# Delta stage: a tile's q, k, v and z in three transfers, three slots for solved blocks, the last substitution spread over the rounds

## What is computed

```
def step(S, inp):
    qc, kc, vc, gc, bc = inp
    decay = jnp.exp(jnp.where(incl, gc[..., :, None] - gc[..., None, :], -jnp.inf))
    kbeta = kc * bc[..., None]
    a = jnp.where(strict, jnp.einsum('bhid,bhjd->bhij', kbeta, kc) * decay, 0.0) + eye
    rhs = jnp.concatenate([vc * bc[..., None], kbeta * jnp.exp(gc)[..., None]], axis=-1)
    sol = lax.linalg.triangular_solve(a, rhs, left_side=True, lower=True, unit_diagonal=True)
    u, w = sol[..., :DV], sol[..., DV:]
    v_new = u - jnp.einsum('bhck,bhkv->bhcv', w, S)
    attn = jnp.einsum('bhid,bhjd->bhij', qc, kc) * decay
    o = (jnp.einsum('bhck,bhkv->bhcv', qc * jnp.exp(gc)[..., None], S)
         + jnp.einsum('bhij,bhjv->bhiv', attn, v_new))
    g_last = gc[..., -1]
    S = (S * jnp.exp(g_last)[..., None, None]
         + jnp.einsum('bhck,bhcv->bhkv', kc * jnp.exp(g_last[..., None] - gc)[..., None], v_new))
    return S, o
```

## Time and profile before

| | |
|---|---|
| time, median of 3 runs | 5176.89 us (5173.43 to 5181.04) |
| profiled execution, its own time | 5176.11 us |
| its span in the trace | 5174.5 us |
| delta stage in the trace | first instruction 854.28, next stage's first transfer 1353.15 us |
| TensorE products, busy share of the whole span | 86% |
| VectorE, ScalarE, POOL | 36%, 31%, 15% |

### The profile page before, as it was taken

How to read it: one execution, slowest core, us unless ns; L and a number is a source line. 1 busy time by engine, 2 the same in 40 slices (tenths; PEclk the granted TensorE clock), 3 DMA queues, 4 the chain that set the end, 5 groups by cost and what they waited for, 6 DMA issues and landing times. The chain is left out here.

```text
span 5174.5 us, 84659 instructions
## 1 busy us (share of the span) xinstructions
PE 4428.8 (86%) x33347; PEld 4164.1 (80%) x33347; DVE 1882.2 (36%) x2633; ACT 1627.9 (31%) x2867; POOL 778.8 (15%) x567
## 2 busy tenths in 40 slices
PE   5799995767696999899778888479999999999994
PEld 4789995666695999898545668369999999999993
DVE  3455664544212000111112222234445454455454
ACT  2574331434322000122102222144334344444441
POOL 0234310211232232133000003100000000000001
PEclk6899997988897999999888558689999999999996
DMA  1223487445431122234010002175556666676675
GB/s 42 59 71 96 132 221 173 116 110 128 117 115 54 62 69 67 67 105 126 31 46 1 0 0 65 70 204 164 155 163 174 172 179 176 176 197 178 178 210 176
DMA packets 1048766, 600.88 MB, mean 116 GB/s; under 512 B 184465, under 2 KB 1006194, under 8 KB 1048578
## 3 DMA queue, kind: packets, MB, share of 16 engines
q1 hardware_dynamic: 984114, 524.46, 36.7%
q10 hardware_dynamic: 55344, 46.60, 3.1%
q0 software_dynamic: 9120, 27.24, 1.7%
HBM read 498.56 MB, written 99.26 MB: 116 GB/s over the span
## 5 line engine op out<-in xcount | busy, mean ns | idle before, releaser
L2247 DVE TENSOR_TENSOR experts_w<-experts_raw,experts_w 128x1024 fp32r<-128x1024 f32 x352 | 415.4, 1221 | 153.6 <-ACT experts_w L2207 153.5
L182 PE MATMUL experts_pa<-experts_hx,experts_w 128*128 128x264 f32 (+6 forms) x1408 | 413.0, 293 | 9.1 <-DVE experts_w L2247 9.1
L183 PE MATMUL experts_pa<-experts_hx,experts_w 128*128 128x264 f32 (+6 forms) x1408 | 411.5, 292 | 0.0
L184 PE MATMUL experts_pa<-experts_hx,experts_w 128*128 128x264 f32 (+6 forms) x1408 | 410.4, 291 | 0.0
L182 PE MATMUL experts_pd<-experts_hid,experts_w 128*128 128x264 f32 (+6 forms) x1408 | 410.2, 291 | 0.0
L183 PE MATMUL experts_pb<-experts_hx,experts_w 128*128 128x264 f32 (+6 forms) x1408 | 409.6, 291 | 0.0
L182 PE MATMUL experts_pb<-experts_hx,experts_w 128*128 128x264 f32 (+6 forms) x1408 | 409.2, 291 | 0.0
L183 PE MATMUL experts_pd<-experts_hid,experts_w 128*128 128x264 f32 (+6 forms) x1408 | 408.9, 290 | 0.0
L184 PE MATMUL experts_pb<-experts_hx,experts_w 128*128 128x264 f32 (+6 forms) x1408 | 408.7, 290 | 0.0
L184 PE MATMUL experts_pd<-experts_hid,experts_w 128*128 128x264 f32 (+6 forms) x1408 | 408.6, 290 | 0.0
L182 PE MATMUL proj_pm<-hT,proj_w_hi 128*128 128x384 f32 (+1 forms) x1152 | 389.6, 338 | 18.4 <-POOL proj_w_lo L622 18.4
(11 more groups left out here) (383 smaller groups left out, 10365.2 us busy)
## 6 DMA issues: line engine op xcount, KB each, us to landing
experts_raw<-in_moe_w SPq DMA_DIRECT2D x352, 512.0 KB, 4.7
experts_raw<-in_moe_w SPq DMA_DIRECT2D x128, 704.0 KB, 6.0
projected<-proj_out SPq DMA_DIRECT2D x48, 544.0 KB, 4.1
proj_w<-in_gdn_w_in ACTq DMA_DIRECT2D x48, 512.0 KB, 4.1
ffnup_w<-in_ffn_w SPq DMA_DIRECT2D x44, 512.0 KB, 4.9
ffndown_w<-in_ffn_w SPq DMA_DIRECT2D x32, 704.0 KB, 4.7
mixout_w<-in_gdn_w_out SPq DMA_DIRECT2D x32, 512.0 KB, 4.1
hidden<-ffnup_hid ACTq DMA_DIRECT2D x22, 544.0 KB, 2.7
```

The costliest lines, as they stand in the source:

```text
L182: pe.matmul(out, as_r(w_hi), as_r(x_hi), start=first, stop=False)
L183: pe.matmul(out, as_r(w_hi), as_r(x_lo), start=False, stop=False)
L184: return pe.matmul(out, as_r(w_lo), as_r(x_hi), start=False, stop=last)
L2247: dve.tensor_tensor(as_r(w[:, u, 1, x, 0:KD, :]), raw[:, x, u, 0:KD, :], w[:, u, 0, x, 0:KD, :], ALU.subtract).then_inc(split[x][u], 1)
```

## The change

- TT, BT and their semaphores get three slots (`AHEAD`), taken by c modulo 3; between and solved blocks of chunk c+3 instead of c+2 are loaded in round c, between ahead of solved. Three clearings stand at the start.
- `load_tile` issues three transfers, v, q with k, and z, each 16 heads of 128 frames, in runs of 512 bytes, into tiles that hold all heads. Tile 0 and the sample's state are issued by ScalarE at its start, the other tiles by SyncE as before.
- POOL's `stage` copies a chunk's v and k (k twice, by a broadcast read) into kst and vst, which now hold two chunks; v and k are turned from there. The products with the state read k and q in the new tile, the gate reads z there.
- The last group's substitution is cut into eight pieces of two rows, one in each of rounds 0 to 7, at VectorE's x0. It is stored in round 11.
- `delta_chunks` is written with a lag between the chains, which is 0.
- The stage has nine more semaphores.

The diff, cut to its core:

```
-def substitute(dve, step, blocks, solved, terms, groups):
+def substitute(dve, step, blocks, solved, terms, groups, first=1, end=SUB):
...
-    for i in range(1, SUB):
+    for i in range(first, end):
...
+LAG = 0
+AHEAD = 3
...
+    n = len(ORDER)
+    for at in range(-n, n * (NCHUNK + 1) + LAG * CHAINS):
+        for ch in range(CHAINS):
+            now, step = divmod(at - LAG * ch, n)
+            run(ch, now, ORDER[step])
...
+        qk, v, z = (st.sb(n, [P, 2, HV, P]) for n in ("qk", "v", "z"))
+        kst, vst = each("kst", [P, 2, PAIRS, 2, CHUNK]), each("vst", [P, 2, HC, CHUNK])
...
-        BT = st.sb("BT", [P, 2, L, HK, CHUNK])
-        TT = st.sb("TT", [P, 2, 2, HK, CHUNK])
+        BT = st.sb("BT", [P, AHEAD, L, HK, CHUNK])
+        TT = st.sb("TT", [P, AHEAD, 2, HK, CHUNK])
...
+            def load_tile(eng, t):
+                par, n = t % 2, TILES[t][1]
+                for to, first, loaded in ((v, 2 * HK, v_loaded), (qk, 0, qk_loaded), (z, 2 * HK + HV, z_loaded)):
+                    eng.dma_start(to[:, par, :, 0:n], proj[first:first + HV, :, t * P:t * P + n].rearrange("h p t -> p h t")).then_inc(loaded[par], 16)
...
+                load_between(0)
                 load_solved(0)
-                load_between(0)
-                load_tile(0)
-                load_solved(1)
-                load_between(1)
                 load_own(0)
-                load_own(1)
                 src = m["block_dram"].rearrange("a k hp i g f -> (a k hp i) g f")
                 sp.dma_start(blocks[:, 0, :, :].rearrange("p j i -> p (j i)"), src[:, NT - 1, :]).then_inc(blocks_loaded, 16)
-                load_tile(1)
...
+                load_between(1)
+                load_solved(1)
+                load_own(1)
+                load_between(2)
+                load_solved(2)
+                load_tile(sp, 1)
                 for c in range(NCHUNK):
                     if c and c % 2 == 0:
                         for ch in C:
                             sp.wait_ge(sems[ch]["o_gated"], PRE + c)
                         store_out(c // 2 - 1)
                         if c // 2 + 1 < NT:
-                            load_tile(c // 2 + 1)
+                            load_tile(sp, c // 2 + 1)
+                    if c == LAST - 2 - AHEAD:
+                        sp.wait_ge(flip_ready, PRE + 1)
...
+                    if c + AHEAD < NCHUNK:
+                        load_between(c + AHEAD)
+                        load_solved(c + AHEAD)
                     if c + 2 < NCHUNK:
-                        load_solved(c + 2)
-                        load_between(c + 2)
                         load_own(c + 2)
...
+                    t = tile(c)
+                    pool.wait_ge(v_loaded[t], landed(c))
+                    if c >= 2:
+                        pool.wait_ge(e["v_turned"], PRE + c - 1)
+                        pool.wait_ge(e["k_turned"], PRE + c - 1)
+                    pool.tensor_copy(vst[ch][:, c % 2, :, :], v[:, t, HC * ch:HC * ch + HC, cols(c)]).then_inc(e["v_staged"], 1)
+                    pool.wait_ge(qk_loaded[t], landed(c))
+                    pool.tensor_copy(kst[ch][:, c % 2, :, :, :], qk[:, t, HK + PAIRS * ch:HK + PAIRS * ch + PAIRS, cols(c)].unsqueeze(2).broadcast_to([P, PAIRS, 2, CHUNK])).then_inc(e["k_staged"], 1)
...
+                load_tile(act, 0)
+                for ch in C:
+                    act.dma_start(S[ch][:, 1, :, :], io["state_delta"][0, 0, HC * ch:HC * ch + HC].rearrange("h k v -> k h v")).then_inc(sems[ch]["state_loaded"], 16)
...
-                substitute(dve, step, blocks, solved, terms, 1)
-                dve.tensor_copy(flipped[:, 0, :, :], solved[:, 0, :, :].rearrange("p r c -> p c r")).then_inc(flip_ready, 1)
+                def last_group(ch, c, l):
+                    if ch or l or not 1 <= c <= SUB // 2:
+                        return
+                    if c == 1:
+                        dve.wait_ge(blocks_loaded, PRE + 16)
+                    substitute(dve, step, blocks, solved, terms, 1, 2 * c - 1, min(2 * c + 1, SUB))
+                    if c == SUB // 2:
+                        dve.tensor_copy(flipped[:, 0, :, :], solved[:, 0, :, :].rearrange("p r c -> p c r")).then_inc(flip_ready, 1)
```

## The result

The changed kernel takes 5030.74 us (median of four runs, 5026.76 to 5039.29) against 5176.15 of the kernel before beside it (5173.43 to 5181.04): a ratio of 0.972, 95% interval 0.9703 to 0.9737. 5034.0 us had been forecast. The profiled execution of after took 5030.56 us with a span of 5028.9, 145.6 less than that of before.

A forecast was written before the change was run, and what follows sets the result against it. Late solved blocks, queued behind tiles on SyncE, stall TensorE, which otherwise bounds the delta rounds. The terms -117.1 - 2.3 - 28 + 4 + 1.3 sum to -142.1, taking 5176.1 to 5034 us, range 5020 to 5075.

The forecast's parts named there:

- What bounds the kernel: Delta stage: TensorE waits for late solved blocks behind tile issue on SyncE; rounds without the stall are bound by TensorE.
- (a): Delta rounds, three slots for solved and between blocks: all 15 waits go, intervals 276.7 instead of 393.8 us, -117.1.
- The seventh cold restart: Last stretch of the delta stage, from 1307.15 us: TensorE's restart at a lower clock goes too, -2.3 us.
- (f): Nine more semaphores, set and cleared: at most 0.16 us each, twice; 0 to 2.9 us, taken as +1.3.
- (b): SyncE's tile in three transfers: issue takes 12 to 14 us, taken as 13, instead of 16.65; none on the path.
- the new runs do nothing, and the sum stands: Rival on SyncE's tile issue: it stays at 16.65 us and the forecast sum holds; no chance of its own given.
- The loads keep the pace: Rival, chance 0.14: queue, landing or contention bring SyncE's pair of rounds above 37 us; 5064 us.
- (c): Regrouping on POOL: four copies a round, 0.62 us each, cost 0 as long as one takes less than about 2 us.
- The rival by which copies set the round: POOL's chain, 9.6 + 4t, passes 18.5 us at 2.2 us a copy; 5202 us at 5 us; chance 0.04.
- (d): Substitution spread over rounds 0 to 7 on VectorE: multiplies blocked by POOL cost 0 to 9 us, taken as +4.
- (e): Stage start: VectorE no longer delays TensorE, while ScalarE issues tile 0 and state; gain 20 to 33 us, taken as -28.
- The signs: Delta-stage trace: x0 of chunk 1 near 885, chunk 16 near 1166, intervals 18.0 to 19.5 us, no wait above 2.

The follow-up runs named there:

- e3: The changed kernel with all 15 steps of the last group's substitution again ahead of VectorE's first step, blocks still loaded early; 5047.84 us.
- e8: The changed kernel with ScalarE issuing only v and qk of tile 0, z and the state following on SyncE; 5030.26 us, ratio to before 0.9719.
- e1: The kernel before with three slots for solved and between blocks, loads three chunks ahead, and nothing else of the change; 5074.91 us.
- e9: The changed kernel with each of a tile's three transfers cut into two half tiles, so runs of 256 bytes; 5045.10 us.
- e6: The changed kernel with each regrouping copy on POOL done five times in a chain; 5067.33 us.
- e5: The changed kernel with each spread piece of the substitution done three times; 5053.56 us.
- e2: The changed kernel with two slots again (AHEAD 2), all the rest of the change kept; 5114.29 us.

## Why the prediction was right, step by step

**What bounds the kernel** held. The 15 waits were those of the second slot: with three slots and nothing else 110.3 us of the stage go, with everything but the slots waits of 6 to 12 us stay.

**(a)** -117.1 forecast, -114.5 measured. The 2.6 us are mostly four rounds that are longer than 18.43 (19.79, 19.42, 19.03 and 18.71). The first three hold a gap in the middle of d0 for which the trace names no engine (1.09, 0.73 and 0.34 us):

```profile
946.47 0.27 PE L1067 MATMUL delta_bank_x<-delta_TT,delta_X 64*64 64x64 f32 x2 [1.09 <-issue]
```

They come ahead of chunks 5, 9 and 13; e3 and e8 have their longer intervals at the same chunks, and one more ahead of chunk 15. No run was made on their cause; it stays open. The seventh cold restart (-2.3 forecast) lies between X(15) and the landing of the last outputs: 38.90 us before, 37.22 after, 1.7 less, and the granted clock over the first 18 us of it is 0.90 before and 1.00 after. The 0.9 by which the last stretch grows behind that landing belong to (f).

The **cover** that (a) rests on was counted too generously. I put SyncE's pair at 18 us plus the tile: 34.6 with the old tile. Three slots alone gave 38.4 to 40.1 with a tile of 16.0 to 17.3, short runs 37.0 to 42.6 with one of 15.0 to 15.9. So what lies beside the tile is 22.3 us on average in e1 and 23.6 in e9, not 18: behind a tile `BT` takes 0.9 to 2.9 us to issue and 16 pieces 7.5 to 10.3 in these two kernels, where I had put 0.5 and 7.44. With this the tile's 16.65 us would not have fitted, and (b) is part of the gain.

**(b)** The issue of a tile takes 8.3 to 9.8 us, less than my 13; of what it saves, `BT` and the pieces behind it take back 2 to 3 (25.3 on average beside the tile in after, 22.3 and 23.6 with the long tiles). The pair takes 34.3 where I had 31. v lands 9.0 and qk 11.3 us behind their issue, as put down. The rival "the new runs do nothing, and the sum stands" fell in its second half: had they done nothing, short runs show what follows, 10.0 us more in the rounds and 7.3 at the start. "The loads keep the pace" was nearer than its 14% said: its mechanism is that of e1 and e9, and after escapes it by the 1.7 to 4.4 us that SyncE stands idle in a pair.

(The text speaks of 18 transfers for a tile's q, k, v, z; there are 16, as the kernel's description says. No number hangs on it.)

**(c)** A copy takes 612 ns, forecast 0.62, and costs nothing:

```profile
L1025 POOL COPY delta_kst<-delta_qk 128x512 f32<-128x512 f32 x34 | 20.8, 612 | 4.2 <-DMA delta_qk<-projected 4.2
L1023 POOL COPY delta_vst<-delta_v 128x512 f32<-128x512 f32 x34 | 20.8, 612 | 2.7 <-DMA delta_v<-projected 2.7
```

The waits of 4.2 and 2.7 us are the start's; no copy waits in the rounds. The rival by which copies set the round was right in its mechanism and too dear by 2.2 us in its constant (e6).

**(d)** +4 forecast, 0 measured. The collision is there, as one piece of after in VectorE's list and POOL's beside it show:

```profile
997.79 4.08 POOL L1033 TENSOR_TENSOR delta_S<-delta_S,glast 128x1024 f32<-128x1024 f32 x2 [9.89 <-PE delta_bank_s L1097]
...
1000.14 0.33 DVE L425 TENSOR_REDUCE delta_solved<-delta_terms 128x13 f32<-128x169 f32 x1
1000.50 1.72 DVE L424 TENSOR_TENSOR delta_terms<-delta_solved,delta_blocks 128x196 f32<-128x196 f32 x1
1002.25 0.36 DVE L425 TENSOR_REDUCE delta_solved<-delta_terms 128x14 f32<-128x196 f32 x1
1002.65 1.41 DVE L1239 SCALAR_TENSOR_TENSOR delta_out<-delta_bank_s,gains,delta_z 128x512 f32<-128x512 f32 x2
1003.97 1.27 DVE L1189 TENSOR_TENSOR delta_TT<-delta_TT,delta_bank_x 128x512 f32<-128x512 f32 x2
```

The second multiply takes 1.72 us where e3, with POOL idle, has 0.49. So it is with the second multiply of each round from 0 to 6, 1.56 us for 4 elements to 1.72 for 196. The first one is not held but holds POOL: in rounds 0 to 7, as it grows from 0.15 to 0.54 us, the two scalings beside it grow from 3.78 to 4.18, and in round 8, without a piece, they take 3.75. Blocked once, for the second scaling, and not for a copy as well, a piece ends 1.2 to 1.4 us later, and the cover just holds that: in round 6 some 0.2 us of it are left (e5). So the term's place was right and its size lay at its lower bound: e3, without the pieces, has rounds of 279.48 against 279.28. (The rule of the Trainium skill, "SBUF — State Buffer", "Who interferes with whom", that such a pair excludes each other for a whole instruction, agrees with the 1.72 us here; the +9 that I derived from it does not, since the exclusion fell on time that nobody was waiting for.)

**(e)** -28 forecast, -29.75 measured, but the reason given was not the one that held. I had x0 at 864.5 and ScalarE busy issuing until 870.5. In after x0 waited for its own block until 874.10, 15.82 us behind the first clearing, while ScalarE was through with issuing at 872.50 and its first copy, at 875.26, waited for nothing but x0. What held x0 was the landing: 16 engines at a share of 1.10 [the third stretch above] with two queues full, and pieces that took 6.5 us to land instead of the 1.8 of the earlier trace rows. Two errors of about 5 us met: x0 later than thought, ScalarE off the path. The first copy, put down for 16.2 us behind the first clearing, came at 17.0, but held by x0 and not by ScalarE's issuing. That the landing is what delays x0 is seen against before and e1, where tile 0 is not on ScalarE's queue: there the 16 pieces had landed 9.7 us behind the first clearing, in after only at 15.6. e8, with 2 MB less, moves x0 by only 1.75 us, and by 1.2 to 1.4 against e2, e3, e5 and e6, which have after's queue (15.2 to 15.5). e9 shows the other case, where ScalarE does hold the chain, by 7.5 us. The size came out right by luck; the cause was wrong.

**(f)** +1.3 forecast, +1.6 measured. The first clearing comes 4.00 us later, but 3.3 of that had arisen before the landing of the project stage's last solved blocks. From that landing to the first clearing it takes 10.07 us in before, 10.30 in e1 (three semaphores more), 10.54 in e2 (six), 10.77 or 10.78 in after, e3, e5, e8 and e9 (nine) and 10.85 in e6 (ten): 0.08 us for each, +0.7 in after. At the other end, from the landing of the last outputs to the next stage's first transfer, it is 7.11, 7.30, 7.79 and 7.98 us in the same order (7.75 in e6): +0.9 in after. So the term was right in its place, twice, and nearly in its size.

**The signs.** x0 of chunk 1 at 887.6 (near 885), x0 of chunk 16 at 1166.9 (near 1166), clock 1.00, no wait above 2 us, POOL's copies 0.61, multiplies of 1.6 to 1.7 us: all there. The intervals, 17.9 to 19.8 where I had 18.0 to 19.5, have two of fifteen just outside. The one that came out the other way was ScalarE, free at 872.5, short of the 875 that would have been wrong, yet later than the 870.5 of the step. The measured sum is -145.6 against -142.1: (a) 2.6 and the cold restart 0.6 less, (f) 0.3 dearer, (d) 4 and (e) 1.8 more, and what lies ahead of the handover and behind the stage 1.2 more. That the sum came within 3.5 us is in part these errors cancelling.

## What to carry to other kernels

A further slot turns a wait per period into a question of throughput: add up everything that the issuing queue does in a period, at the durations which it has when full, and compare it with the bound engine's period. Here it was 34.3 of 36.9 us. Against after, the stage kept 77.5 us with two slots, 17.3 with runs of 256 bytes and 34.8 with the slots alone, of which 6.4 in the rounds and the rest mostly at the start. Read several periods of the queue, not one: in e9 they went from 37.0 to 42.6 us. Where work is tucked into an engine's spare time, do it twice or thrice in an experiment: that shows how much cover there is, and what each us past it costs, the clock included.

## What the hardware showed that was not expected

- The time to issue is not a property of the transfer. The same `BT` (512 KB) took 0.35 to 3.75 us in after, 16 pieces of 8 KB 8.2 to 10.3, a tile of 3 MB 8.3 to 9.8 in runs of 512 bytes and, in e9, 15.0 to 15.9 in runs of 256. What one transfer saves, those queued behind it pay back in part.
- A copy with one input was blocked by POOL too: the turned copy of the solved block took 1.54 us beside a scaling in after and 0.37 alone in e3, while a reduction took the same beside POOL's scaling as without it (0.33 us for 169 elements, at 1000.14 in after and at 876.23 in e3, with POOL idle). The two rows of the copy, after first:

```profile
1019.16 1.54 DVE L1252 COPY delta_flipped<-delta_solved 128x256 f32<-128x256 f32 x1
...
878.51 0.37 DVE L1247 COPY delta_flipped<-delta_solved 128x256 f32<-128x256 f32 x1
```

- A wait of TensorE can cost more than itself: 1.79 us in e1 came with a granted clock of 0.92 over that round, which was 2.75 us longer than the one before it; 3.67 us in e5 with 0.88 in the stretch behind it and a round 5.48 us longer than after's. The length of the one wait does not decide it: after 1.92 us in e5 the round's clock stayed at 1.00.
